# A hybrid streaming layer with 64 experts on one core: eight instead of five expert pairs get their rows by an indirect transfer

## The reference

```python
def _moe(x, w_router, router_bias, exp_w1, exp_w3, exp_w2, sh_w1, sh_w3, sh_w2):
    ...
    _, eidx = lax.top_k(jnp.where(emask, sb, -jnp.inf), TOP_K)        # 8 of 64 experts for a token
    wsel = jnp.take_along_axis(s, eidx, axis=1)
    wsel = wsel / jnp.sum(wsel, -1, keepdims=True) * ROUTED_SCALE
    gates = jnp.einsum('tk,tke->te', wsel, jax.nn.one_hot(eidx, N_EXPERTS, dtype=jnp.float32))
    ...
        hid = jax.nn.silu(jnp.einsum('td,edf->tef', tb, exp_w1)) * jnp.einsum('td,edf->tef', tb, exp_w3)
        return jnp.einsum('tef,efd->td', hid * gb[..., None], exp_w2)
    ...
    shared = (jax.nn.silu(t @ sh_w1) * (t @ sh_w3)) @ sh_w2
    return (routed + shared)
```

## Time and profile before

| what | value |
|---|---|
| median of 3 runs | 1506.17 us (1506.12 to 1508.46) |
| the profiled execution's own time | 1506.84 us |
| its span | 1505.1 us |
| TensorE busy | 1459.8 us, 97% |
| VectorE, ACT, POOL busy | 648.7, 389.6, 116.7 us |
| moved by DMA | 375.27 MB, mean 249 GB/s |
| chain that ended last | PE 82%, DVE 7%, DMA 4%, ACT 2% |

### The profile page before, as it was taken

How to read it: one execution, slowest core, us unless ns; L and a number is a source line. 1 busy time by engine, 2 the same in 40 slices (tenths; PEclk the granted TensorE clock), 3 DMA queues, 4 the chain that set the end, 5 groups by cost and what they waited for, 6 DMA issues and landing times.

```text
span 1505.1 us, 31065 instructions
## 1 busy us (share of the span) xinstructions
PE 1459.8 (97%) x13071; PEld 1011.3 (67%) x13071; DVE 648.7 (43%) x1225; ACT 389.6 (26%) x873; POOL 116.7 (8%) x107
## 2 busy tenths in 40 slices
PE   7999999999999999999999999999999999999994
PEld 6776677677776777767667765767575766676751
DVE  5223787875644677735541114522212121111237
ACT  2112444342322454435430101111111111111111
POOL 3000113121010000000000000000101000000000
PEclk9999999999999999999999999999999999999998
DMA  7778375563344544564567538599999999999985
GB/s 243 168 171 180 103 213 165 127 206 99 104 129 147 138 111 116 177 181 162 147 222 270 157 107 363 230 364 403 419 425 428 428 429 428 427 428 427 428 346 159
DMA packets 157033, 375.27 MB, mean 249 GB/s; under 512 B 101724, under 2 KB 110316, under 8 KB 139232
## 3 DMA queue, kind: packets, MB, share of 16 engines
q1 hardware_dynamic: 123904, 341.42, 64.2%
q10 hardware_dynamic: 26416, 15.41, 3.5%
q0 software_dynamic: 6576, 16.48, 3.2%
HBM read 327.14 MB, written 51.95 MB: 252 GB/s over the span
## 4 chain that ended last, share of the span: by engine, by line
PE 82%; DVE 7%; DMA 4%; ACT 2%; DVEq 2%; issue 1%; ACTq 1%; SPq 0%
PE PS L576 25%; PE PS L1069 14%; PE PS L919 9%; PE PS L1036 7%; PE PS L1088 7%; PE PS L624 3%; DVE region L1493 2%; DVE region L1486 2%; PE PS L1041 2%; PE PS L957 2%; DMA region<-expert_rows 2%; PE PS L632 1%; PE PS L1052 1%; ACT L1172 1%; PE PS L1077 1%
## 5 line engine op out<-in xcount | busy, mean ns | idle before, releaser
L576 PE MATMUL PS<-h0T,region 128*128 128x320 f32 x1808 | 510.7, 437 | 1.2 <-issue 0.8
L576 PEld LDWEIGHTS PS<-h0T,region 128*128 128x128 f32 x1808 | 336.8, 190 | 145.5 <-issue 13.0
L1172 ACT ACTIVATE region<-PS 128x9 f32<-128x9 f32 (+6 forms) x407 | 148.5, 382 | 681.5 <-PE PS L576 312.6
L1069 PE MATMUL PS<-region 128*64 128x512 f32 x1024 | 228.8, 592 | 0.0
L1069 PEld LDWEIGHTS PS<-region 128*64 128x64 f32 x1024 | 124.4, 137 | 92.2 <-issue 32.0
L1486 DVE TENSOR_TENSOR region<-region 128x256 f32<-128x256 f32 (+10 forms) x210 | 127.6, 627 | 96.7 <-ACTq L1215 76.2
L919 PE MATMUL PS<-region 128*128 128x320 f32 x512 | 138.3, 433 | 1.5 <-DMA region<-wo 1.4
L919 PEld LDWEIGHTS PS<-region 128*128 128x128 f32 x512 | 97.1, 190 | 42.3 <-issue 2.1
L1172 ACT ACTIVATE region<-region 128x256 f32<-128x256 f32 (+8 forms) x160 | 81.1, 530 | 154.6 <-DMA region<-projected 39.0
L1172 ACT ACT_TABLE_LOAD x80 | 102.6, 1283 | 70.1 <-DMA region<-projected 54.4
L1088 PE MATMUL PS<-region,history 128*64 128x512 f32 x512 | 119.7, 596 | 0.8 <-ACTq L1451 0.5
(11 more groups left out here) (208 smaller groups left out, 1166.8 us busy)
## 6 DMA issues: line engine op xcount, KB each, us to landing
region<-moe_w SPq DMA_DIRECT2D x64, 2048.0 KB, 17.3
region<-moe_w SPq DMA_DIRECT2D x64, 1024.0 KB, 15.2
region<-w_in SPq DMA_DIRECT2D x115, 512.0 KB, 5.6
region<-wo SPq DMA_DIRECT2D x32, 512.0 KB, 3.6
projected<-region ACTq DMA_DIRECT2D x65, 167.5 KB, 4.0
expert_rows<-region SPq DMA_DIRECT2D x20, 512.0 KB, 7.3
region<-expert_rows SPq DMA_DIRECT2D x4, 2048.0 KB, 13.7
region<-projected SPq DMA_DIRECT2D x10, 768.0 KB, 6.3
```

What stands on the lines that cost most here:

```text
L576: last = mm(PS[:, 6 + i % 2, 0:NTOK], WR[:, i, k, :], H0T[:, k, :], start=(k == 0), stop=(k == KT - 1))
L1069: last = mm(PS[tiles(i), 2, :], XE[:, k, tiles(i)], W13[r][i][:, k * 512:k * 512 + 512], start=(k == 0), stop=(k == KT - 1))
L1172: return nc.scalar.activation(out, in_, f, **kw)
```

## The change

`FETCHED`, the list of fetched pairs, goes from five (every fifth pair from 6 to 26) to eight (every third from 6 to 27). The one-hot rows of the fetched pairs (`OHF`) and their table of gates, places and numbers (`INFOF`) lie elsewhere in the tile `h0T`; the table has grown from 90 to 144 columns.

```diff
-FETCHED = (6, 11, 16, 21, 26)
+FETCHED = (6, 9, 12, 15, 18, 21, 24, 27)
...
-        XR, OHF = HT[:, 0:D], shaped(HT[:, 2 * D:2 * D + 384], 3, 128)
-        INFOF = shaped(HT[:, 2 * D + 384:2 * D + 474], 3, len(FETCHED), 2, 3)
+        XR, OHF = HT[:, 0:D], shaped(HT[:, D:D + 384], 3, 128)
+        INFOF = shaped(HT[:, 2 * D:2 * D + 18 * len(FETCHED)], 3, len(FETCHED), 2, 3)
```

## The result

| | before | after |
|---|---|---|
| median of 9 runs, same chip | 1506.17 us (1505.32 to 1509.75) | 1513.72 us (1510.71 to 1518.62) |
| ratio | | 1.0052, 95% interval 1.0041 to 1.0063 |
| profiled execution, own time (span) | 1506.84 us (1505.1) | 1516.24 us (1514.4) |

The change makes the kernel 0.52% slower, 7.6 us by the medians. The forecast was 1507.3 us, no measurable change. The profiled execution of after lies 2.5 us above its median, so its rows show somewhat more delay (9.4 us against before's) than most runs have.

What follows compares the result with a forecast made beforehand. It took the DMA engines as the bound: three fetches delay weights and vectors 3.7 us to 1456.8, partly offset by filling a tail hole; rows land 1.1 us later, so 1506.17 + 1.1 = 1507.3 us, range 1502.5 to 1510.5.

Steps and rivals of the forecast that it cites:

- TensorE's gain: Expert stage: three pairs transposed instead of gathered save 11.2 us, preparations take 3.4, so TensorE ends 7.8 us sooner.
- the rival in which TensorE sets the end: Expert stage: loads have hidden slack and everything moves with TensorE, -7.8 us, 1498.4 us; chance of over 3 us faster 0.13.
- The places: Setup and tile: moving the one-hot rows and lengthening the setup copies' vectors costs nothing.
- step (4): POOL's queue in the expert stage: three more fetches take 1.2 us each of all 16 engines, 3.7 us in all.
- Pair 27's weights: Late expert stage: wanted at 1385.8, landing at 1384.8, leaving 1.0 us of the former 12.5.
- Step (7): Tail: vectors land at 1456.8, six loads of rows follow without a gap, last rows at 1486.9, 1.1 us later.
- step (2): Ahead of pairs 6, 7 and 8: three more preparations cost TensorE 3.4 us, including a 1.7 us wait for VectorE.
- Step (6): Expert stage: TensorE asks for weights sooner, but never-empty engines serve in order; they land no sooner and TensorE hardly stalls.
- the middle: Tail: 1486.9 for the last rows' landing, between 1487.4 by the last engine and a lower end of 1486.4.
- The tail's clock: Tail: TensorE's clock halves after an 8 us pause, +9 us, 1515.5 us; chance 0.12 of over 3 us slower, including dearer fetches.
- The range: Whole kernel: own range 1503.6 to 1508.8 us, widened into the other cases to 1502.5 to 1510.5.
- the bounds: Fetch under a full queue: nothing, 1.2 us by bytes, or 1.7 us each, giving -2.6 to +2.6 us at the end.

Runs made afterwards that it cites:

- e4: The changed kernel without the fetches of pairs 9, 15 and 24, which are transposed from whatever rows are in the tile: 1510.14 us, 1.0032 against before.
- e1: Before with only the one-hot rows and their table moved, still five fetches: 1506.06 us, ratio 1.0003.
- e2: Before with three more fetches of 128 rows each into an unused part of the tile: 1508.78 us, ratio 1.0016.
- e15: Before with its five preparations spread over rounds 1, 5, 10, 15, 20 and the last rows in one 128-partition load: 1500.58 us, 0.9965.
- e16: The changed kernel with its eight preparations spread over rounds 1 to 23 and the last rows in one 128-partition load: 1503.14 us, 0.9978 against before.
- e9: The changed kernel with its last three preparations moved from rounds 6, 7, 8 to 8, 11, 14: 1512.33 us, 1.0048 against before.
- e7: The changed kernel with pair 6 gathered again, so seven fetched pairs and seven preparations: 1517.51 us, 1.0072 against before.
- e11: The changed kernel with the two last 64-partition loads held back until the fourth load of rows has landed: 1511.71 us, 1.0038 against before.
- e12: The changed kernel with one 128-partition load in place of the two last 64-partition loads: 1505.96 us, 0.9996 against before.
- e6: Before with the second of the two last 64-partition loads issued from ACT's queue: 1505.57 us, ratio 1.0000.
- e5: The changed kernel with the second of the two last 64-partition loads issued from ACT's queue: 1512.09 us, 1.0043 against before.
- e3: Before with eight preparations instead of five, the fetched pairs unchanged: 1510.32 us, ratio 1.0029.
- e14: Before with its five preparations spread over rounds 1, 5, 10, 15 and 20: 1504.49 us, ratio 0.9987.
- e13: Before with one 128-partition load in place of the two last 64-partition loads: 1503.79 us, ratio 0.9982.

## Why the prediction was wrong

**Right.** That the DMA engines are the bound and TensorE's gain goes into waits: the rival in which TensorE sets the end (1498.4 us) is refuted by the result and by e4, which has the shorter rounds without the fetches and is still 0.32% above before. The places cost nothing that can be told (e1). The fetches cost about what step (4) said, 3.7 us: 2.4 to 3.4 in e2, 3.0 by e4, 2.6 between e15 and e16. Pair 27's weights were to have 1.0 us of slack, and TensorE waited 1.34 us for them: nearly right in sum, but by two misses that partly offset each other. TensorE was only 5.6 us ahead there, not 7.8 (it would have begun at 1388.1), and the weights landed at 1389.6, 8.5 us later than before and not 3.7.

**The step that failed is (7), the tail:** "the other five as long as before, 1485.8 - 1460.1 = 25.7". They took 1494.7 - 1465.2 = 29.5 us. It sits in the fourth load, 10.0 us instead of 5.8; the second and third together took 10.6 instead of 9.6, the halves 8.9 instead of 10.3. The sum took the six loads as a fixed train behind the vectors. It isn't one: the halves overlap the load ahead of them. The first half landed 1.1 us before the fourth load (2.8 in e9, 2.1 in e7), and while halves are written the full share moves only 203 to 209 GB/s. e11 and e12 show both sides: no halves in flight, or none at all, and rows 4 take 4.9 us. The likely reason is that some of the 16 engines are ahead of the others at the end of the weights and start on the halves while the others still have rows 4 to do. That the two loads of vectors, 0.5 MB each, land 7.9 us apart (1452.4 and 1460.3; before 1445.4 and 1453.2) fits it, but no row shows single engines, so this part is argued. The sign of it stood in the trace of before: the window 1474 to 1482 at share 1.00 and 209 GB/s, next to a window at 430. I took the last landing (24.36 us after its issue) into the sum and did not ask at what rate it was reached.

The Trainium skill (SBUF — State Buffer, "Can I just issue two DMAs to hit both halves?") states that transfers to the lower and the upper 64 partitions do not add up to the rate of one over 128. The rows here agree: 209 GB/s with both under way from two queues in e6, 203 to 209 with both in SyncE's queue, against 4.9 us, 430 GB/s, for the same bytes in e12.

**Step (7) also began too late by 3.5 us,** which is a wrong size of steps (2) and (6). The vectors landed at 1460.3, not 1456.8. Step (6) called the engines "never empty", but from 1076 to 1160 they moved 1.1 MB (2.6 us) less; the other 0.9 us isn't traced. The preparations in front of pairs 6 to 8 cost TensorE some 5.5 us, not 3.4: L1108 waited 1.75 us, and the 31 matmuls behind it took 8.76 us where 32 usually take 7.04. The first is what step (2) said, 1.7. The second is TensorE's clock:

```profile
1074.00:1076.00 2.00, 2.00 (x8) 1.15 (x6) 0.00 (x0) 0.00 (x0) 0.00 (x0) 0.50 1.00 426
```

After the wait of 1.75 us the granted clock was 1.00 until about 1072.6, then 0.50, the lower of its two levels (1.2 GHz), until 1076, while TensorE was busy; this is where the 1.7 us went. e5 and e11 have the same fall and the same 8.76 us, behind waits of 1.80 and 2.01 us. e3, e4 and e12, which waited 1.56, 1.14 and 1.33 us there, stayed at 1.00 and have 7.06 us. The prediction looked for the clock in the tail alone. So TensorE freed the ring later just when the queue was shortest. By e9 this hole decides little in the change itself: closing it gave 0.04%, below what can be told. Whether the clock falls in pair 6's matmuls in most executions of the change isn't known; there is the trace of one execution. On before, where the loads are less behind, spreading the preparations gave 0.13% (e14).

The last rows of the profiled execution are thus 1494.7 instead of 1486.9: 3.5 us by the vectors, 3.8 by the loads behind them, and 0.5 because I took the middle between 1487.4 and 1486.4. Against before that is 8.9 us, and with the 0.6 us that the last sum took longer it makes the 9.4 us of the profiled executions.

**What a faster TensorE triggers.** Step (7) granted the loads of rows a start at 1444.4, 7.8 us sooner. They went out at 1452.6, before 1452.2. Pair 29's scatter was issued at 1440.9, 4.1 us sooner, and took 11.6 us, before 7.0: the DMA share there is 0.89, before 0.58. So the tail took back what TensorE had left of its lead. Over the stage VectorE waits for scatters 100.2 us in 17 waits, before 70.0 in 13, though they land as fast as before (median 10.4 us in both): the short rounds leave them less time.

**The tail's clock.** TensorE's windows show that the granted clock fell in the pause:

```profile
1470.00:1472.00 2.00, 0.92 (x1) 0.50 (x2) 1.80 (x3) 0.00 (x0) 0.00 (x0) 0.50 0.97 418
```

0.50 is the lower level again, after 7.9 us without work; from 1474 to 1476 the mean is 0.66, and from 1476 on it is 1.00. L1099 took 5.79 us instead of 3.70, inside a stretch in which TensorE then waited for the last rows; the last sum took 5.91 instead of 5.35 (3.60 in e12, which has no pause ahead of it). So this rival costs 0.6 us, not the 9 of its working: its mechanism happened, its condition (more than 8 us of work at the lower level) did not. It had the right sign and nearly the right time (1515.5 us) for a reason that was not the cause.

**The range** ended at 1510.5 because the bounds priced only the three fetches. Even there the upper bound of a fetch was worked out wrongly: 5.6 us over three fetches are 1.9 us each, not 1.7, so the range's own end was 1509.3 and not 1508.8. The unknown that mattered was the tail's rate, and it had no bound.

**Open.** That some engines are behind the others at the end of the weights is argued, and why they would be isn't shown; the rows of the trace are of whole transfers. Nor is it shown why the fourth load takes 9.7 to 11.2 us in the versions with eight or seven transposed pairs and 5.4 to 7.1 in those with five. It isn't the added fetches (e2 has 7.1 us with them, e4 9.7 without) and not the early hole (e9, 9.9); what is left in common is that TensorE is early and the queue is long: the fourth load lands 26 to 32 us after its issue in these versions, 15 to 19 in the others. And e3 gives three more preparations 0.3% where e9, which moves them, hardly gives any back: that their cost, too, passes through the halves fits e12 and e13 but wasn't tried by itself.

## What to carry to other kernels

Read the DMA rate beside its share: a full share at half the rate is a slow kind of transfer, and it can also slow what is queued ahead of it. Where the DMA engines bound a stage, time saved on a compute engine turns into waits, and the bytes that bought it are paid for. A train of loads in a tail isn't a constant: before it is carried over as one sum, look at which loads overlap and at what rate each runs.

## What the runs showed of the hardware

Two loads over 64 partitions each, one behind the other, run at 203 to 209 GB/s with a DMA share of 1.0; by themselves (e11) 2.1 MB took 12.9 us from the first issue; the same bytes over 128 partitions land 4.9 us after the load ahead. A load of 2.1 MB over 128 partitions with such halves right behind it landed 5.4 to 11.2 us after the one before it, without them 4.8 to 4.9; a half can land before the load that was issued ahead of it (1484.6 against 1485.7). Both halves under way from two engines' queues ran at the same 209 GB/s (e6, 1.0000). The indirect fetch of 128 rows of 4 KB cost 0.8 to 1.1 us of a full queue. TensorE's granted clock fell to 0.50 soon after a wait of 1.75 us ahead of pair 6's matmuls, and 31 of these took 8.76 us instead of 7.06.
